# Two-block transformer kernel on one core: VectorE's order at three stage entries (copies out of PSUM, products and weight rests ahead of input sums and gate steps)

## The reference, cut to what matters

```python
def conv_ffn(h, norm_g, w_gate, w_up, conv_w, conv_b, w_down):      # first block, both layers
    xn = rms_norm(h, norm_g)
    a = xn @ w_gate                                                  # 1024 -> 2816
    a = conv_b + conv_w[0]*shift(a, 2) + conv_w[1]*shift(a, 1) + conv_w[2]*a
    return (silu(a) * (xn @ w_up)) @ w_down

def swiglu(hn, w_ffn_in, w_ffn_out):                                 # second block
    a, b = split(hn @ w_ffn_in, 2)
    return (silu(a) * b) @ w_ffn_out

def hgrn2_mixer(h, norm_g, w_in, lower_bound, o_gain, w_out):        # first block, layer 1
    q, f_logit, i, g = split(rms_norm(h, norm_g) @ w_in, 4)
    f = lb + (1 - lb) * sigmoid(f_logit)
    q, k, log_f, v = silu(q), 1 - f, log(f), i                       # 8 heads of 128
    # S_t = diag(f_t) S_{t-1} + k_t v_t^T ;  o_t = S_t^T q_t, in chunks
    return (rms_norm(o, o_gain) * sigmoid(g)) @ w_out
```

## Time and profile before

| What | Value |
|---|---|
| median of 3 runs | 2759.65 us (2759.45 to 2760.19) |
| profiled execution, its own time | 2761.77 us |
| span of its profile | 2760.1 us |
| PE busy | 2699.0 us (98%), 18315 matmuls |
| DVE busy | 1816.7 us (66%) |
| ACT busy | 1363.3 us (49%) |
| POOL busy | 303.9 us (11%) |
| mean granted TensorE clock | 0.995 of full |
| stage entries in the change | mixer 770 to 812, feed-forward 1 1158 to 1197, SwiGLU 2405 to 2439 us |

### The profile page before, as it was taken

The page is one execution under the profiler, slowest core; times in us unless marked ns, Lnnn a source line. Parts: engine busy times, 40 slices in busy tenths (PEclk is TensorE's granted clock), DMA queues, the critical chain, the costliest instruction groups (busy, mean ns, idle before and its releaser), DMA issues.

```text
span 2760.1 us, 50224 instructions
## 1 busy us (share of the span) xinstructions
PE 2699.0 (98%) x18315; PEld 2458.0 (89%) x18315; DVE 1816.7 (66%) x2928; ACT 1363.3 (49%) x2400; POOL 303.9 (11%) x268
## 2 busy tenths in 40 slices
PE   7999999999999999999999999999999999999998
PEld 6898899999989999899988888887899988789986
DVE  6777757886367776678853453553677775688832
ACT  4455445664245554556642223232478884455632
POOL 2000012330022211023201011010000000100000
PEclk9999999999999999999999999999999999999999
DMA  4222225884221111268833222223312222223332
GB/s 127 69 73 60 58 77 131 173 183 107 85 80 54 53 53 46 80 144 178 169 105 112 85 71 85 87 68 88 90 56 61 61 61 84 84 79 104 108 94 73
DMA packets 458589, 252.62 MB, mean 92 GB/s; under 512 B 9221, under 2 KB 452870, under 8 KB 458486
## 3 DMA queue, kind: packets, MB, share of 16 engines
q1 hardware_dynamic: 414550, 211.45, 27.0%
q0 software_dynamic: 43152, 37.01, 7.5%
q10 hardware_dynamic: 784, 2.75, 0.3%
HBM read 249.05 MB, written 2.13 MB: 91 GB/s over the span
## 4 chain that ended last, share of the span: by engine, by line
PE 61%; DVE 6%; issue 2%; ACT 2%; DVEq 0%; ACTq 0%; POOLq 0%; POOL 0%
PE ps L529 24%; PE ps L533 13%; PE ps L926 13%; PE ps L1138 2%; PE ps L1296 2%; PE ps L1337 1%; DVE wl L496 1%; PE ps L1326 1%; PE ps L1358 1%; PE ps L1263 1%; PE ps L1416 1%; PE ps L1183 1%; PE ps L1249 0%; PE ps L1330 0%; DVE rl L3105 0%
## 5 line engine op out<-in xcount | busy, mean ns | idle before, releaser
L496 DVE TENSOR_TENSOR wl<-raw,wh 128x1024 fp32r<-128x1024 f32 (+3 forms) x309 | 366.9, 1188 | 292.3 <-ACT wh L492 289.8
L492 ACT ACTIVATE wh<-raw 128x1024 fp32r<-128x1024 f32 (+3 forms) x309 | 303.8, 985 | 387.0 <-PE ps L529 211.9
L533 PE MATMUL ps<-xh,wh 128*128 128x264 f32 x1856 | 390.0, 291 | 7.2 <-DVE xl L563 5.9
L533 PE MATMUL ps<-xl,wh 128*128 128x264 f32 x1856 | 378.8, 285 | 0.0
L533 PE MATMUL ps<-xh,wl 128*128 128x264 f32 x1856 | 378.3, 285 | 0.0
L533 PEld LDWEIGHTS ps<-xh,wh 128*128 128x128 f32 x1856 | 290.0, 189 | 15.6 <-issue 6.4
L533 PEld LDWEIGHTS ps<-xl,wh 128*128 128x128 f32 x1856 | 289.0, 189 | 0.0
L533 PEld LDWEIGHTS ps<-xh,wl 128*128 128x128 f32 x1856 | 288.3, 189 | 0.0
L529 PE MATMUL ps<-xh,wh 128*128 128x512 f32 x512 | 208.0, 406 | 7.0 <-DVE wl L496 6.1
L529 PE MATMUL ps<-xl,wh 128*128 128x512 f32 x512 | 203.8, 398 | 0.0
L529 PE MATMUL ps<-xh,wl 128*128 128x512 f32 x512 | 202.6, 396 | 0.0
(11 more groups left out here) (469 smaller groups left out, 6640.7 us busy)
## 6 DMA issues: line engine op xcount, KB each, us to landing
raw<-in_w_in SPq DMA_DIRECT2D x88, 512.0 KB, 3.8
raw<-in_ffn_w_gate SPq DMA_DIRECT2D x44, 512.0 KB, 5.5
raw<-in_ffn_w_up SPq DMA_DIRECT2D x44, 512.0 KB, 4.9
raw<-in_w_ffn_in SPq DMA_DIRECT2D x44, 512.0 KB, 3.7
raw<-in_fox_w_in SPq DMA_DIRECT2D x33, 512.0 KB, 4.2
raw<-in_hgrn_w_in SPq DMA_DIRECT2D x32, 512.0 KB, 4.0
raw<-in_ffn_w_down SPq DMA_DIRECT2D x32, 448.0 KB, 3.7
raw<-in_ffn_w_up POOLq DMA_DIRECT2D x36, 256.0 KB, 6.7
```

The costliest lines, as they stand in the source:

```text
L492: nc.scalar.activation(wh[:, v % 2, 0:nk, :], raw[:, v % RAW_SLOTS, 0:nk, :], ACT.Copy).then_inc(s("w_hi"), 1)
L496: nc.vector.tensor_tensor(wl[:, v % 2, 0:nk, :], raw[:, v % RAW_SLOTS, 0:nk, :], wh[:, v % 2, 0:nk, :].bitcast(F32), ALU.subtract).then_in ...
L533: last = nc.tensor.matmul(ps[:, bank + b, 0:HALF], w[:, slot, kk, :], x[:, k0 + k, b * HALF:(b + 1) * HALF], start=first, stop=end_)
```

## The change

On DVE alone, three pieces of the hand-written order:

- feed-forward stage 1: `x_sums(2)` moves from before `product_classic(0, 0)` to after the rest of the next weight unit (`split_ahead(..., 0, 2)`);
- SwiGLU: `product_classic(0, 0)` moves before `x_sums(0)`; `x_sums(2)` moves from before `gate_classic(0, 1)` to after `product_classic(0, 1)` and the rest of the next unit (`split_ahead(..., 1, 1)`), which itself moves before `hid_lo(0)`;
- mixer: the copy of `g_v` moves from after the query's `sigmoid_log` to before the rest of the next weight unit.

Feed-forward stage 0 keeps its order. No instruction is added or removed, on any engine, and no DMA is moved.

```diff
@@ up_duo, n < 2 @@
                 conv_rest(0, 0)
-                x_sums(2)
+                if n == 0:
+                    x_sums(2)
                 product_classic(0, 0)
                 split_ahead(dve, dve_lo, PH_UP[n], 0, 2)
+                if n == 1:
+                    x_sums(2)
                 hid_lo(0)
@@ up_duo, n == 2 @@
                 split_ahead(dve, dve_lo, PH_UP[n], 1, 0)
-                x_sums(0)
                 product_classic(0, 0)
-                x_sums(2)
+                x_sums(0)
                 gate_classic(0, 1)
                 product_classic(0, 1)
-                hid_lo(0)
                 split_ahead(dve, dve_lo, PH_UP[n], 1, 1)
+                x_sums(2)
+                hid_lo(0)
                 gate_classic(1, 0)
@@ mixer @@
         hgrn_running(0)
+        scaled_out(PH_HGP, 0, 2, g_v[:, :])
         split_ahead(dve, dve_lo, PH_HGP, 0, 2)
         sigmoid_log(q_x, q_e, q_e, 0, "q_below", "q_logs")
-        scaled_out(PH_HGP, 0, 2, g_v[:, :])
```

More of the change, by code:

```diff
@@ L2602, in up_duo @@
                 split_ahead(dve, dve_lo, PH_UP[n], 1, 0)
+                product_classic(0, 0)
                 x_sums(0)
-                product_classic(0, 0)
-                x_sums(2)
                 gate_classic(0, 1)
                 product_classic(0, 1)
+                split_ahead(dve, dve_lo, PH_UP[n], 1, 1)
+                x_sums(2)
                 hid_lo(0)
-                split_ahead(dve, dve_lo, PH_UP[n], 1, 1)
                 gate_classic(1, 0)
```

## The result

| Kernel | Median, us | Lowest to highest |
|---|---|---|
| before | 2759.55 | 2758.28 to 2760.81 (6 runs) |
| changed | 2771.12 | 2767.97 to 2773.30 (6 runs) |

The ratio is 1.0036, with a 95% interval of 1.0026 to 1.0045: 9.9 us slower (7.2 to 12.4). The forecast was 3.8 us slower, with an upper end of 2766.8. The direction was right; the size lies outside the range. The changed kernel's profiled execution took 2770.77 us, its span is 2769.1, 9.0 over the span of before.

What follows compares the result with a forecast made beforehand. TensorE, busy 98% of the span, was taken as the bound, so only its waits and half clock count. The terms 0.3 + 0.75 + 1.4 + 1.35 + 0 = 3.8 us slower gave 2763.4 us, range 2758.3 to 2766.8.

Steps and rivals of the forecast that it cites:

- Stage 1: Feed-forward stage 1: wait of 2.99 us becomes 1.1, a new 4.1 us wait follows, group starts 0.75 us later.
- SwiGLU: SwiGLU stage: waits of 0.89 and 1.11 us gone, the 1.96 us wait grows to 5.8; net 1.35 us later.
- The mixer: Mixer entry: copy of `g_v` starts some 2.3 us earlier, yet pick and PE come 0.3 us later (0 to 1.3).
- the gate: Stage 1 and SwiGLU: ACT's `x_rounded` waits for all input sums, starting 1.75 and 1.35 us later, delaying PE's weights.
- the rule: Mixer: two-SBUF-input DVE steps and POOL exclude each other; POOL ends at about 788.9, loss 0.28 us, without the rule 1.3.
- the price of the clock: Stage 1: half clock likely after the 4.1 us wait, costing 1.4 us, bounds 0 and 1.6.
- how the sum was carried to the median: Whole program: 3.8 us slower, profiled execution to 2765.6 us, against the median of 2759.65 forecast as 2763.4.
- Rival D: Delays grow: stretched DVE steps stay at the mixer, stage 1 rest, loads and adding transfers late; 2766.4 us, chance 0.10.
- B: Stage 1 and SwiGLU: `x_rounded` isn't what PE's weights wait for; 8.8 us faster, 2750.9, chance 0.06.
- C: Only the clock differs: no fall in stage 1, none any longer at mixer and SwiGLU; -0.8 us, 2758.9, chance 0.12.

Runs made afterwards that it cites:

- ffn1_act_first: ffn1_only with ACT's rounding of the next weights put ahead of `x_rounded`; 2761.95 us, ratio 1.0004.
- after_keep: Changed kernel with 16, 15 and 22 matmuls that nobody reads filling most of PE's three long waits; 2763.23 us, ratio 1.0006 to before.
- mixer_tuned: Kernel before, mixer only: `q_e` step, then copy of `g_v`, ahead of the weight rest, and head 0's first two picks moved ahead; 2759.96 us, ratio 0.9993.
- swiglu_only: Kernel before with the change's SwiGLU part alone; 2763.53 us, ratio 1.0010.
- the two filled kernels: Changed kernel and kernel before, each with unread matmuls put in PE's long waits; 2763.23 us (1.0006) and 2760.81 us (0.9998).
- ffn1_only: Kernel before with the change's feed-forward stage 1 part alone; 2763.57 us, ratio 1.0013.
- the three single parts: Kernel before with one edit of the change each: mixer 2764.63 us (1.0015), stage 1 2763.57 (1.0013), SwiGLU 2763.53 (1.0010).
- swiglu_split: Kernel before with only the SwiGLU entry reordered on DVE and ACT, and PE's one wait for 23 parts of x made three; 2759.81 us, ratio 1.0002.
- tuned_all: Kernel before with all three entries reordered: ACT roundings and DVE rests in stage 1, mixer picks ahead, SwiGLU sums and rests later; 2756.84 us, ratio 0.9983.
- before_again: Kernel before, unchanged, profiled a second time; 2763.02 us in this one execution.
- mixer_picks: Kernel before with the change's mixer part and head 0's first two picks ahead of the weight rest and `hgrn_left`; 2759.93 us, ratio 0.9998.
- tuned3: Kernel before with mixer_tuned's mixer entry, tuned_all's stage 1 order, and swiglu_split's SwiGLU order and three waits; 2754.27 us, ratio 0.9981.

## Why the prediction was wrong

**The mechanisms stood.** Stage 1: the wait of 2.99 us became 1.07 (1.1 said), then 4.09 came one group later (4.1), and the group starts 0.77 us later from the entry's own start (0.75). SwiGLU: two waits gone and the third 5.89 us (5.8). The mixer: 0.80 at the copy, 4.20 at the pick (4.2 said in the sum of the clock), 0.2 later (0.3). `x_rounded` is the gate, as ffn1_act_first shows.

The Trainium skill, "SBUF — State Buffer", section "SBUF: two separate sides", was weighed in the prediction. The trace after agrees: once POOL's steps were through, `q_e` took 0.70 us in place of the 1.57 of the earlier trace rows, the rest ahead of it 1.43. POOL's last step ended at 788.14, which is 788.93 on the time axis of before's first profile (whose starts at 780 us lie 0.79 us later); by the rule it was to end at about 788.9.

**The step that failed** is the price of the clock: "Its price is what the rows at half clock cost over those at full: 7.20 - 5.8 + 0.2 for the tail = 1.6 us", with "Bounds 0 and 1.6". Those rows show falls that came when PE was working again, 3.4 us of half clock each. In the longer waits of the changed kernel the clock fell while PE still stood, and stayed down for 6.8 us. Of that, 5.9 us lay behind the end of the wait at the mixer, 5.5 in stage 1 and 3.3 at SwiGLU, against 3.4 in those rows. By after_keep the price was 2.7 us at the mixer (none was in the sum), 2.4 in stage 1 (1.4 said), and at SwiGLU 1.5, which before pays too where its clock falls. Against the first profile of before this accounts for 1.0 at the mixer (1.33 for 0.3) and 1.15 at stage 1 (3.30 for 2.15).

**The second failure** is in how the sum was carried to the median, "It lies 2.1 us above the median of the runs, and against that median of 2759.65 the forecast is": the changed kernel's profiled execution lay 0.35 us below its median, not 2.1 above. The sum was made against one execution's course. That profile showed the dear course at two entries, a fall behind the pick wait and one at SwiGLU, 1.6 us each, which the usual execution doesn't have (six of seven, and five of eight). By these counts, which come from profiles of several kernels, the change costs more against the median than against that profile: 2.5 to 2.9 at the mixer, 3.3 at stage 1 and 2.4 at SwiGLU (1.43 plus five eighths of 1.6), 8.2 to 8.6 in all. The measured 9.9 (7.2 to 12.4) holds that.

**Chance** made the first pair of profiles look as far apart as the medians: 1.51 us by the fall at 1138 and 2.04 in the seven-product part, of which 1.6 went with a wait of ACT for one adding transfer, in the trace after:

```profile
1287.85 0.63 ACT L1476 ACTIVATE wh<-w_sum1a 128x512 fp32r<-128x512 f32 x1 [2.70 <-DMA w_sum1a<-in_ffn_w_up]
```

Such waits stand in kernels with no edit in stage 1 too (2.99 us more in mixer_tuned, 2.00 in swiglu_only), so they need no change. Whether the change makes them more frequent stays open: the column from 1200 to 1511 has a mean of 1.2 us in the seven profiles with the old order at stage 1 and of 2.2 in the eight in which it was moved, the two filled kernels left out. Rival D had named them with 1 us.

**The rivals.** B (8.8 faster) and C (the clock spared) did not occur. D came nearest in size and had other grounds: the stretched DVE steps did not stay.

Left open: why an execution takes one course or the other at the same 3.22 us wait, and the 1.3 to 1.7 us between 8.2 to 8.6 and the measured 9.9, which lie within the interval.

## What to carry to other kernels

Where the busiest engine is at 98%, an edit of order is worth the waits it moves and the clock behind each: a wait that grew from 2 or 3 us to 4 or more cost up to 2.7 us beyond its own shift, and the price went with the half clock left behind the wait's end, not with the wait's length (5.89 us cost 1.5). In ffn1_act_first the same wait, cut to 2.79 us, passed without a fall. Follow the piece that is moved back to whoever waits for it (here ACT's one pass for sixteen sums), and mend that place in the same edit; where the queue has no gap, as DVE's at SwiGLU, order only chooses the place of the wait. And before a sum goes by one profile, ask of each of its clock falls whether the next execution would have it.

## What was not expected of the hardware

The half-clock stretches had two lengths only, but for the one that runs into the program's end. Summed over windows, 3.4 us: at 803, 1172, 2383 and 2431 us in before, at 64 and 1139 in after, at 792 in ffn1_only. 6.8 us: the three entries of the changed kernel in both profiles, and the same places of the three single parts. Past the first 60 us, all that began after the wait's end were short (in the start-up some of 6.8 us began 1.3 to 1.6 us behind a wait, as at 19 us in after). So were those that began up to 0.6 us ahead of it: at 2383 in before, at 2438.7 in swiglu_split (its 3.06 us wait ended at 2439.3), at 2432.7 in tuned_all. Those that began 0.8 us or more ahead of it were long.

What a fall costs can be read at a wait that no edit touches. In all 17 profiles PE waits 5.1 us at the start of the SwiGLU stage, and the clock falls within the wait, 0.1 to 3.1 us ahead of its end. In before:

```profile
2384.06 0.77 PE L1416 MATMUL ps<-xh,wh 128*128 128x512 f32 x1 [5.09 <-DVE xl L563]
```

The half clock left behind the wait's end runs from 2.8 us (before) to 6.0 (ffn1_only), and the table's column from 1511 to 2400 us from 0 to 1.38 with it: 0.43 us for each us of half clock, no profile more than 0.15 off that line. The entries come near it: 2.7, 2.4 and 1.5 us for 5.9, 5.5 and 3.3 us left.

The same wait of 3.22 us for `g_v` passed without a fall (before), had one of 3.4 us behind it (before_again), and one of 6.8 us that began within it (ffn1_act_first, tuned_all). Where it cost PE 1.5 or 3 us the next wait took nearly all of it back, since DVE's picks set the end: 780 to 900 us took -1.58 and -1.53. Waits of 2.71, 2.79 and 3.08 us passed free in one profile each (mixer_picks, ffn1_act_first, tuned3). By the Trainium skill, "TensorE: Matmul & The Clock Gate", section "What's actually happening", the number of matmuls that a kernel runs at the low clock at its start differs from run to run; these traces show the same for waits in its middle.
